# Column sums for the conditioning: four 128x128 transposes and a vector reduction, or four products with one column of ones

## The reference, cut to what matters

```
def adaln(cond, w_ada, b_ada):
    return jnp.split(jax.nn.silu(cond) @ w_ada + b_ada, ADA_CHUNKS, axis=-1)
...
m_lat = [m[:, None, :] for m in adaln(c, w_ada[l], b_ada[l])]
m_ctx = adaln(c_ctx, w_ada[l], b_ada[l])
hc = modulate(rms_norm(ctx, norm1_g[l]), m_ctx[0], m_ctx[1])
h = modulate(rms_norm(x, norm1_g[l]), m_lat[0], m_lat[1])
```

## Time and profile before

| | us |
|---|---|
| median of 3 executions | 2930.0 |
| the profiled execution | 2927.9 |
| its span, first to last instruction | 2926.1 |
| TensorE matmul busy in it | 2864.7 |
| TensorE weight load busy | 2368.7 |
| VectorE busy | 1964.3 |
| ScalarE busy | 1330.5 |
| GpSimd busy | 23.5 |

### The profile page before, as it was taken

One profiled execution on the slowest core, in us unless ns is written; L12 is line 12 of the kernel. 1 busy time (PEld: TensorE's weight loads), 2 busy tenths in 40 slices (PEclk: granted clock), 3 DMA queues, 4 the chain that ended last, 5 costly groups with the idle time before them and its releaser, 6 DMA issues.

```text
span 2926.1 us, 34632 instructions
## 1 busy us (share of the span) xinstructions
PE 2864.7 (98%) x13645; PEld 2368.7 (81%) x13645; DVE 1964.3 (67%) x2525; ACT 1330.5 (45%) x1651; POOL 23.5 (1%) x47
## 2 busy tenths in 40 slices
PE   8899999999999999999999999999999999999999
PEld 8888788888888887788888777778878888888887
DVE  5775588989878667753347777767766555655444
ACT  5445454444444446532334455554444444444333
POOL 2000000000000000000000000000000000000000
PEclk9999999999999999999999999999999999999999
DMA  7444577787778887533346565647757777776564
GB/s 230 129 125 146 164 244 245 247 252 250 255 255 269 269 267 237 172 101 96 92 139 186 171 181 177 183 132 255 238 180 222 223 225 223 224 228 207 189 192 153
DMA packets 299954, 583.23 MB, mean 199 GB/s; under 512 B 18393, under 2 KB 18801, under 8 KB 299152
## 3 DMA queue, kind: packets, MB, share of 16 engines
q1 hardware_dynamic: 297472, 573.06, 63.2%
q0 software_dynamic: 2320, 7.96, 0.9%
HBM read 578.85 MB, written 2.10 MB: 199 GB/s over the span
## 4 chain that ended last, share of the span: by engine, by line
PE 91%; DVE 5%; ACT 2%; issue 1%; DMA 0%; SPq 0%; ACTq 0%; DVEq 0%
PE psum L505 21%; PE psum L508 21%; PE psum L507 21%; PE psum L566 3%; PE psum L568 3%; PE psum L567 3%; PE psum L2776 2%; PE psum L2778 2%; PE psum L2777 2%; PE psum L478 2%; PE psum L480 1%; PE psum L2794 1%; PE psum L481 1%; PE psum L2804 1%; PE psum L527 1%
## 5 line engine op out<-in xcount | busy, mean ns | idle before, releaser
L623 DVE TENSOR_TENSOR w_lo<-w_raw,w_hi 128x1024 fp32r<-128x1024 f32 x720 | 877.8, 1224 | 589.4 <-ACT w_hi L617 585.2
L617 ACT ACTIVATE w_hi<-w_raw 128x1024 fp32r<-128x1024 f32 x720 | 762.8, 1060 | 1042.9 <-PE psum L508 1039.0
L505 PE MATMUL psum<-w_hi,x_split 128*128 128x512 f32 x1984 | 782.9, 395 | 4.3 <-issue 3.1
L508 PE MATMUL psum<-w_hi,x_split 128*128 128x512 f32 x1984 | 776.1, 391 | 0.0
L507 PE MATMUL psum<-w_lo,x_split 128*128 128x512 f32 x1984 | 775.4, 391 | 0.0
L505 PEld LDWEIGHTS psum<-w_hi,x_split 128*128 128x128 f32 x1984 | 373.9, 188 | 81.1 <-issue 5.8
L508 PEld LDWEIGHTS psum<-w_hi,x_split 128*128 128x128 f32 x1984 | 373.7, 188 | 78.3
L507 PEld LDWEIGHTS psum<-w_lo,x_split 128*128 128x128 f32 x1984 | 374.2, 189 | 75.3
L505 PE MATMUL psum<-w_hi,hidden_split 128*128 128x512 f32 x704 | 275.3, 391 | 0.0
L508 PE MATMUL psum<-w_hi,hidden_split 128*128 128x512 f32 x704 | 274.4, 390 | 0.0
L654 DVE SCALAR_TENSOR_TENSOR stat<-w_raw,conditions,stat 128x512 f32<-128x512 f32 x360 | 269.8, 749 | 6.8
(11 more groups left out here) (355 smaller groups left out, 3405.3 us busy)
## 6 DMA issues: line engine op xcount, KB each, us to landing
w_raw<-in_w_in SPq DMA_DIRECT2D x216, 512.0 KB, 3.7
w_raw<-in_w_ada SPq DMA_DIRECT2D x192, 512.0 KB, 4.8
w_raw<-in_w_ffn_up SPq DMA_DIRECT2D x176, 512.0 KB, 4.5
w_raw<-in_w_ffn_down SPq DMA_DIRECT2D x88, 512.0 KB, 5.6
w_raw<-in_w_ff_gate SPq DMA_DIRECT2D x88, 512.0 KB, 4.4
w_raw<-in_w_ff_up SPq DMA_DIRECT2D x88, 512.0 KB, 4.4
w_raw<-in_w_ff_down SPq DMA_DIRECT2D x88, 512.0 KB, 4.4
w_raw<-in_w_out SPq DMA_DIRECT2D x64, 512.0 KB, 4.6
```

The lines of the kernel that those rows point to most:

```text
L505: nc.tensor.matmul(to, x_hi[:, tokens], hi, start=u == 0 and t == 0, stop=False, skip_group_check=True)
L508: mm = nc.tensor.matmul(to, x_lo[:, tokens], hi, start=False, stop=end and t == 1, skip_group_check=True)
L617: nc.scalar.activation(w_hi[:, b.slot(n)], raw[:, b.raw_slot(k)], ACT.Copy).then_inc(w_rounded, 1)
L623: nc.vector.tensor_tensor(w_lo[:, slot], raw[:, b.raw_slot(k)], r(w_hi[:, slot]), ALU.subtract).then_inc(w_split, 1)
```

## The change

Each transpose becomes a product of the same 128x128 block of the sum, now the stationary operand, with one column of ones. It gives the sums over lanes of 128 columns, one in each lane, in a single column of PSUM. Four such columns lie side by side, and VectorE copies them to MADA in place of summing 512 columns.

```diff
@@ ada_turn
                     for v in range(b.conditions(i)):
                         for f in range(NF):
-                            ins = nc.tensor.transpose(PS[:, 6 + v, f * P:f * P + P],
-                                                      ADA_SUM[v][:, f * P:f * P + P], const("ident"))
+                            ins = nc.tensor.matmul(PS[:, 6 + v, f:f + 1], ADA_SUM[v][:, f * P:f * P + P],
+                                                   const("ones")[:, 0:1], start=f == 0, stop=True,
+                                                   skip_group_check=True)
                     ins.then_inc(ada_turned, 1)
@@ ada_evac
                     for v in range(b.conditions(i)):
-                        ins = nc.vector.tensor_reduce(MADA[:, b.ada_cols[i] * NF:(b.ada_cols[i] + 1) * NF, v],
-                                                      PS[:, 6 + v, :].rearrange("p (f n) -> p f n", f=NF),
-                                                      AX.X, ALU.add)
+                        ins = nc.vector.tensor_copy(MADA[:, b.ada_cols[i] * NF:(b.ada_cols[i] + 1) * NF, v],
+                                                    PS[:, 6 + v, 0:NF])
                     ins.then_inc(ada_evacuated, 1)
```

## The result

| us | before | after |
|---|---|---|
| median of the runs (4 and 4) | 2930.7 | 2947.5 |
| profiled execution | 2927.9 | 2946.6 |
| its span | 2926.1 | 2944.8 |
| TensorE matmul busy | 2864.7 | 2882.4 |
| VectorE busy | 1964.3 | 1948.5 |

The ratio is 1.0059, with a 95% interval of 1.0047 to 1.0071. The forecast was 2944.5 us in a range of 2936 to 2950.

The account below looks back on a forecast made before the run. TensorE's issue was taken as the bound: 28.7 us of products come, 14.1 us of transposes go, +14.6, span 2926.1 to 2940.7; with 1.8 outside and 2.1 to the median, 2944.6, said as 2944.5 us, range 2936 to 2950.

Parts of the forecast that it names:

- TensorE is the bound: Whole kernel: TensorE, busy in 98% of the span, issues without gaps and sets the time; engines feeding it are early.
- A set costs 0.897 us in place of 0.436: Line 453: four one-column f32 products replace four transposes; 28.7 us come, 14.1 us go, +14.6 us.
- The upper bound from the earlier trace: Line 453 products priced at 0.237 us each, from eight between other units: 30.3 us for 128, difference +16.3.
- The kind of instruction decides, the columns don't: On TensorE an f32 product is two records with two weight loads, a transpose one; dropping 127 columns saves nothing.
- Rival 2: On TensorE moving columns set the price, so new sets cost next to nothing: at most -14.1 us, 2915.9 us; 4%.
- the 25 ns: The skill's rule, max(60, 6 + columns) cycles at 2.4 GHz, for one column; the change would save 4 us on TensorE.
- VectorE's relief is nothing: 32 reductions become four-column copies, relieving VectorE of 16.8 us, counted as nothing for the time.
- TensorE's waits at line 453 stay: TensorE's waits for the last partial sum, 2.5 us in three places, are kept; if all went, -2.5.
- I count no loss: Clock stays at its upper level, 2.4 GHz, behind the new one-column products, as behind 16 in a row: 0 us.
- Rival 3: After each of 24 groups, one unit of 12 products runs at 1.2 GHz, 2.7 us longer: +65, some 3010 us; 2%.
- The 2.1 us: The median of the runs stands 2.1 us above the profiled execution, added to 2942.5 to give 2944.6.

Follow-up runs that it names:

- e2: The kernel before, transposes kept, with VectorE copying four columns in place of each reduction: 2930.5 us, 0.9999 times the kernel before.
- e4: The kernel before with every VectorE reduction done a second time into a spare tile: 2932.1 us, 1.0009 times the kernel before.
- e1: The kernel before with each transpose replaced by an f32 product with the 128x128 identity, reductions kept: 2944.3 us, 1.0048 times the kernel before.
- e3: The kernel after with every one-column product issued twice, 256 in place of 128: 2988.2 us, 58.1 over the kernel before.
- e5: The kernel of e1 with every 128-column identity product issued twice: 2975.6 us, 45.5 over the kernel before.
- e7: The kernel after with the last partial sum in rounded 32-bit form, multiplied by two columns of ones in one-record products: 2933.7 us, 1.0008 times the kernel before.
- e8: The kernel after, unchanged, measured again: 2950.1 us, 1.0063 times the kernel before.
- e6: The kernel of e3 with the second condition's products one unit of weights later, and copies a unit later: 2978.0 us, 47.8 over the kernel before.

## Why the prediction was right, and where it was not

- *TensorE is the bound.* Shown from both sides, within the intervals given above: e2 and e4 change VectorE's busy time by -15.6 and +17.7 us and move the time by +0.4 and +2.0; e1, e3 and e5 add TensorE records and the time follows.
- *A set costs 0.897 us in place of 0.436.* Measured 0.906 to 0.916; the sum of this term was +14.6 and is +14.9. Taking the price from an operation of the very same form elsewhere in the trace was what made it so close. The upper bound from the earlier trace rows wasn't needed.
- *The kind of instruction decides, the columns don't.* Shown by e1 (128 columns, the same 0.906) and by e7 (one record, 0.456). Rival 2 is out, and with it, for f32, the 25 ns that follow from the Trainium skill's page "VectorE: DVE Perf Modes", section "The TRN2 errata": it is 0.22 to 0.23 us.
- *VectorE's relief is nothing; TensorE's waits at line 453 stay.* Both held: 2.5 us before and after.
- *The clock: "I count no loss".* This step failed. Rival 3, which I gave 2%, had one unit of 12 products at the lower clock behind each of the 24 groups. The clock does fall behind one-column products in this kernel, but in single stretches that cost about 1.6 us each. The profile after has one at a new group, and two more at places where the change put nothing. I had read one profile's 1.00 behind 16 such products as a property, and it was the state of one execution: 10 of 12 profiles have the dip there.
- *How close the number came is in part luck.* For the profiled execution the forecast was 2942.5 us and 2946.6 were measured, 4.1 us more; 3.8 us is what the products of the sets don't explain, and the dips are most of that. The 2.1 us that I added from the profiled execution to the median were 0.8 in the kernel after, and that hid 1.3 of the 4.1. The same kernel measured 2950.1 in e8, at the very edge of the range of 2936 to 2950, which had little room left for the clock.
- *The dip near 1136 us* has no one-column products of this change within 37 us ahead of it; it follows a wait of 1.88 us that the kernel before has too (1.86), without a dip. It comes in four of the 12 profiles, those of the kernel after, e6, e7 and e8, and not in that of e3, which has as many one-column products as e6, twice those of the kernel after. Why is open, and so is whether the change brings it; both profiles of the kernel after have it, and none of those with transposes or with 128 columns.

## What to carry to other kernels

Where TensorE issues without gaps, count the records that an edit adds to it and price each from start to start, by an instruction of the same form and data type in the trace; neither the duration shown nor the number of columns tells the cost of a small product. A transpose of f32 is one record and an f32 product two, so swapping four transposes for four "cheaper" one-column products doubles their price, and the relief of an engine that waits for TensorE pays nothing back. Look for clock dips behind rows of one-column products, above all where TensorE waited just before them, and in more than one profile.

## What the runs showed of the hardware

- An f32 product of a 128x128 block costs TensorE 0.22 to 0.23 us beside others, with 1 column as with 128 (0.906 us for four in both). In the rounded 32-bit form it is one record and 0.114 us, within 5% of a transpose's 0.109.
- TensorE can be 100% busy in the profile and still drop its clock from 2.4 to 1.2 GHz: eight of eight times behind 3.6 us of one-column products (e3), none of eight behind the same with 128 columns (e5). A wait of 1.63 us followed by 0.9 to 1.8 us of one- or two-column products was also followed by a dip, in all four profiles that have this (after, e6, e7, e8), and in none of the five where the same wait is followed by transposes or by products with 128 columns. A dip isn't a fixed property of its place: the 3.6 us of one-column products of line 2844 have one behind them in 10 of 12 profiles, the 1.8 us of line 2630 at some 243 us in two of 12, and the two profiles of one kernel differ there. The Trainium skill, in "TensorE: Matmul & The Clock Gate", section "Part 1: The HAM clock gate", says that the throttle is set by how busy TensorE has been, with two levels; the two levels agree with the 0.50 and 1.00 here, while "busy" must not be read as the profile's busy time.
